# Prompt attention by head pairs, expert sums by TensorE, input weights loaded one stage earlier

## The chip, the cores and the metric

One Trainium2 chip, one of its cores. The metric is the device time of the kernel in microseconds (us); all data are float32. The core's engines are named as in the profile: PE (TensorE matmul), PEld (TensorE weight load), DVE (VectorE), ACT (ScalarE), POOL (GpSimd) and SP (SyncE, which here only starts DMAs). Each engine takes its instructions strictly in the order of its own list and waits on semaphores that other engines raise.

## What is computed

One layer of a decoder, for a prompt of 1024 tokens and for 8 single-token sequences with a past of 8192. What the change touches, cut from the reference (prompt side):

```python
mod = (silu(c) @ w_ada + b_ada)                    # stage_ada
h @ w_in                                           # stage_in: D 1024 -> 2536 columns

def mla_attend(q_nope, q_rope, k_nope, k_rope, c_kv, key_pos, q_pos, w_uv):   # 8 heads
    s = (q_nope @ k_nope + q_rope @ k_rope) * MLA_SCALE
    s = where(key_pos <= q_pos, s, -inf)
    p = softmax(s)
    ...                                            # p @ values, 64 columns a head

def dsa_attend(q, k_sel, v_sel, sel_pos, valid, q_pos, rel_bias):             # 8 heads
    s = q @ k_sel * DSA_SCALE + bias               # only the 256 selected keys are valid
    p = softmax(s)
    return p @ v_sel                               # 64 columns a head

x = x + gate_a * (concat(mla, dsa) @ w_out)        # stage_out
x = x + gate_f * (sum over 6 experts of gate * y_expert + shared expert)      # stage_combine
```

## The kernel before

`build` runs nine stages one after another, with a barrier of all engines between them: ada, in, index, prompt, sample, out, dispatch, routed, combine. The prompt is handled in `NT` = 8 tiles of 128 tokens; tile `NT` is the 8 samples. A float32 matmul is recorded as two MATMUL instructions, a transpose by the identity as one.

**stage_ada** (L190) streams `w_ada` through `NW` = 4 buffers of 3 MB. **stage_in** (L299) then loads `w_in` as five column groups from SP's list (L349), the second x tile between the first and the second, and after the groups the smaller weights and the third x tile. For each tile PE turns x, multiplies by five groups of `w_in` (`project`, L497), and ACT takes each result out of one of two PSUM banks (`take`, L429). ACT's list has `norm_x(2)`, which needs the third x tile, ahead of `take(0, 0)`.

**attend** (L794) is the last part of the prompt stage. An item `n` is one head of one block of 128 queries: for each block `i` (0 to 7) the 8 heads of MLA (`g` = 0) and the 8 of DSA (`g` = 1), 128 items. Causality is used, so block `i` has w = 128 (i+1) keys. For an item:

- `scores` (PE, L902): query as weights, keys streamed, into PSUM `pS[n % 2]`, two banks an item. It waits for `s_nm` of item n-2, that is, until DVE is done with that pair of banks.
- `scale_and_max` (DVE, L1011, L1016): adds mask or bias, writes `S`, and gives the row's maximum.
- `exps` (ACT, L957): exponential and row sum, into `Pr`.
- `turn` (PE, L912): transposes of `Pr` in groups of up to four, into `pT[group % 2]`; a group needs the copy of the group two before it.
- `evac` (DVE L946 for even groups, ACT L944 for odd ones): copies a group to `PT`.
- `pv` (PE, L923): a 128x128 block of `PT` as weights, 64 columns of values streamed, into `pO[n % 2]`.
- `norm` (DVE, L1021, L1025): reciprocal of the sum, and the scaled result to `O`, stored to `omix` with tokens in rows.

An item has one group when i < 4 and two when i is 4 or more. The order in each list is written out by hand:

```python
# PE                          # DVE                        # ACT
scores(n + 1)                 scale_and_max(n + 1)         exps(n + 1)
turn(n)                       evac(dve, n, 0)              evac(act, n, 1)
pv(n - 1)                     norm(n - 1)
                              select(...)  # one step of the key selection of the next block
```

**stage_out** (L2037): for each tile PE turns the mixed rows (`turn_mix`, L2101), ACT copies them to `mT`, PE multiplies by `w_out` (`out`, L2113), DVE scales and adds x; then the router. `turn_mix(t + 1)` stands ahead of `out(t)`, and SP starts the load of the second tile after the two loads of `w_out`.

**stage_combine** (L2728): for each tile POOL gathers six rows of 4 KB a token, one for each chosen expert (L2749), DVE multiplies each by its gate and adds (L2776, L2778), multiplies by `gate_f` (L2780), POOL adds to `z` (L2756), and ACT starts the store. POOL's list has the addition of tile t ahead of the gathers of tile t+3.

Of the kernel before, what the change touches and what calls it, by code (L numbers as in the profile page):

```python
# [128 lines left out]

def build(nc, T):  # L130
    root = ExitStack()
    with root:
# [33 lines left out]
        for st in (stage_ada, stage_in, stage_index, stage_prompt, stage_sample, stage_out, stage_dispatch, stage_routed,  # L166
                   stage_combine):
            stage_name[0] = st.__name__[6:] + "_"
            if st is stage_out:
                G["z"] = sb("z", [P, NT + 1, D])  # L170
            with ExitStack() as ctx:
                st(nc, T, G, sem, *alloc(ctx))

            nc.clear_and_free_semaphores(list(sem_cache.values()))
            nc.all_engine_barrier()
            sem_cache.clear()
# [13 lines left out]
def stage_ada(nc, T, G, sem, sb, ps):  # L190
# [3 lines left out]
    NW = 4  # L194
# [13 lines left out]
    with nc.Block() as block:  # L208
# [25 lines left out]
        def _(act):  # L234
            act.wait_ge(s_c, 64)
            act.activation(sc[:, :], cs[:, :], ACT.Sigmoid).then_inc(s_sc, 1)

# [61 lines left out]
def stage_in(nc, T, G, sem, sb, ps):  # L299
# [5 lines left out]
    Win = sb("Win", [P, KD, D_IN])  # L305
# [23 lines left out]
    cols = [(0, 512), (512, 1024), (1024, 1536), (1536, 2048), (2048, D_IN)]  # L329
    s_ss, s_rs, s_xn, s_t, s_h, s_p, s_e, s_eps, s_b, s_w2, s_v = (  # L330
        sem("in_" + n) for n in ("ss", "rstd", "xn", "t", "h", "p", "evac", "eps", "b", "weights", "v"))
    s_x, s_wc, s_cs = sem("in_x"), [sem(f"in_w{g}") for g in range(5)], [sem("in_cs0"), sem("in_cs1")]
# [4 lines left out]
    with nc.Block() as block:  # L337
        @block.sync
        def _(sp):
# [8 lines left out]
            for g, (a, b) in enumerate(cols):  # L348
                sp.dma_start(Win[:, :, a:b], T["w_in"][0, :, a:b].rearrange("(k p) n -> p k n", p=P)).then_inc(s_wc[g], 16)  # L349
                if g == 0:  # L350
                    load(1)
# [205 lines left out]
        def _(dve):  # L557
# [99 lines left out]
            root_x(0)  # L657
            root_x(1)
            scale_h(0)
# [134 lines left out]
def attend(nc, T, G, sem, sb, ps, U, thr, FIRST, widths, at):  # L794
# [10 lines left out]
    S = [sb(f"S{i}", [P, SEQ]) for i in range(2)]  # L805
    Pr = [sb(f"Pr{i}", [P, SEQ]) for i in range(2)]
    PT = [sb(f"PT{i}", [P, NT, P]) for i in range(2)]
    O = [sb(f"O{i}", [P, D]) for i in range(2)]
    mx = sb("mx", [P, 4, 2])
    rs = sb("rs", [P, 2])  # L810
    mxp = sb("mxp", [P, 2, 4])
    eq, rank, ones = sb("eq", [P, SEQ]), sb("rank", [P, SEQ]), sb("onesrow", [P, SEQ])
# [4 lines left out]
    names = ("S", "nm", "P", "T", "evd", "eva", "O", "on", "row", "mb", "st", "mx", "v", "fin", "bi")  # L817
    s_S, s_nm, s_P, s_T, s_evd, s_eva, s_O, s_on, s_row, s_mb, s_st, s_mx, s_v, s_fin, s_bi = (sem("at_" + n) for n in names)
# [10 lines left out]
    def by_dve(upto):  # L829
        return (upto + 1) // 2  # L830

    with nc.Block() as block:
        @block.sync
        def _(sp):
            def store(i):
                sp.wait_ge(s_on, 16 * (i + 1))
                sp.dma_start(T["omix"][i * P:(i + 1) * P, :], O[i % 2][:, :]).then_inc(s_out[i % 2], 16)

# [15 lines left out]
            t = bias_rows(T)  # L854
            sp.dma_start(bias[:, :, :], bass.AP(t.tensor, t.offset + P - 1, [[H * 384 - 1, P], [384, H], [1, 2 * P]])).then_inc(s_bi, 16)
# [4 lines left out]
            for i in range(2, NT):  # L860
                sp.wait_ge(s_S, 16 * (i - 1))
# [8 lines left out]
        def _(pool):  # L870
# [4 lines left out]
            for i in range(NT):  # L875
                if i >= 2:
                    pool.wait_ge(s_nm, 16 * (i - 1))
# [8 lines left out]
        def _(pe):  # L886
            def scores(n):
                i, g, h = items[n]
                if g == 0 and h == 0:
# [4 lines left out]
                if n >= 2:  # L894
                    pe.wait_ge(s_nm, n - 1)
                w = widths[i]
                b = 64 * (h % 2)
                q = qm[i % 2][0:QK, h, :] if g == 0 else qd[i % 2][b:b + 64, h // 2, :]
                for z in range(0, w, 512):
                    e = min(z + 512, w)  # L900
                    k = kmT[0:QK, h, z:e] if g == 0 else kdT[b:b + 64, h // 2, z:e]
                    m = pe.matmul(pS[n % 2][z // 512][:, 0:e - z], q, k, start=True, stop=True)  # L902
                m.then_inc(s_S, 1)

            def turn(n):
                pe.wait_ge(s_P, n + 1)
                for gi in range(gfirst[n], gfirst[n + 1]):
                    _, b0, cnt = groups[gi]
                    if gi >= 2:
                        pe.wait_ge(s_evd if gi % 2 == 0 else s_eva, gi // 2)  # L910
                    for b in range(cnt):
                        m = pe.transpose(pT[gi % 2][:, b * P:(b + 1) * P], Pr[n % 2][:, (b0 + b) * P:(b0 + b + 1) * P], c("ident"))  # L912
                    m.then_inc(s_T, 1)

            def pv(n):
                i, g, h = items[n]
                pe.wait_ge(s_evd, by_dve(gfirst[n + 1]))
                if gfirst[n + 1] >= 2:
                    pe.wait_ge(s_eva, gfirst[n + 1] // 2)
                if n >= 2:  # L920
                    pe.wait_ge(s_on, n - 1)
                for j in range(i + 1):
                    m = pe.matmul(pO[n % 2][:, 0:64], PT[n % 2][:, j, :], V[g][:, j, h * 64:h * 64 + 64], start=(j == 0), stop=(j == i))  # L923
# [3 lines left out]
            for n in range(len(items)):  # L927
                if n + 1 < len(items):
# [4 lines left out]
            pv(len(items) - 1)  # L933

        def evac(eng, n, odd):
            for gi in range(gfirst[n], gfirst[n + 1]):
                if gi % 2 == odd:
                    _, b0, cnt = groups[gi]
                    eng.wait_ge(s_T, gi + 1)
                    if n >= 2:  # L940
# [1878 lines left out]
```

## Time and profile before

| | us |
|---|---|
| median of 3 runs (3324.84 to 3331.28) | 3330.16 |
| the profiled execution | 3362.59 |
| its span in the trace | 3360.8 |
| PE busy | 2749.1 (82%) |
| DVE busy | 1640.3 (49%) |
| ACT busy | 1053.7 (31%) |
| POOL busy | 379.3 (11%) |

The profiled execution is one run of its own, recorded by the hardware; its span is the time from the first to the last recorded instruction. Its time is 32 us above the median of the unprofiled runs. Busy shares are averages over nine stages with different limits, so the stage is read, not the average. PE's granted clock is one of two levels, 2.4 GHz (1.0 in the profile) or 1.2 GHz (0.5); over a longer stretch the profile shows their mean.

### The profile page before, as it was taken

What the parts mean: (1) busy time and instruction counts of PE and PEld (TensorE: products, weight loads), DVE (VectorE), ACT (ScalarE), POOL (GpSimd) and SP (SyncE); (2) the same over time, 40 slices, a digit from 0 to 9 for tenths busy, and PEclk for the clock granted to TensorE, in tenths of its full rate; (3) what the DMA queues carried; (4) which work ended last, traced back from release to release, by engine and by line L of the source; (5) the groups of instructions that cost most, each with busy time, mean ns of one, the idle gap of its engine ahead of it and who ended that gap; (6) DMA issues with size and microseconds to landing.
All of it is one profiled execution on the core that took longest, in us unless ns stands there. A gap on an engine that the chain in (4) does not pass through costs nothing. (4 is left out here: it accounts for less than half of the span.)

```text
span 3360.8 us, 42372 instructions
## 1 busy us (share of the span) xinstructions
PE 2749.1 (82%) x14194; PEld 1585.7 (47%) x14194; DVE 1640.3 (49%) x3931; ACT 1053.7 (31%) x2214; POOL 379.3 (11%) x373
## 2 busy tenths in 40 slices
PE   4699996869898989699997447978688899999950
PEld 1344434458786878576775403534233333333310
DVE  0255554668687787656775852267111111111138
ACT  0122223559696877533332001122011111111100
POOL 0000001011000101011010130015100000100037
PEclk8899997879998999857998768989799999999975
DMA  8412225132170202050001124120989977887866
GB/s 323 173 56 79 68 66 217 35 120 75 60 243 20 99 28 76 19 151 29 15 21 68 40 78 167 58 101 13 348 336 339 387 263 289 328 310 262 295 249 223
DMA packets 230771, 514.83 MB, mean 153 GB/s; under 512 B 23269, under 2 KB 84911, under 8 KB 223184
## 3 DMA queue, kind: packets, MB, share of 16 engines
q1 hardware_dynamic: 190580, 344.31, 29.4%
q0 software_dynamic: 29648, 130.76, 10.8%
q10 hardware_dynamic: 10388, 37.79, 2.8%
q8 instruction: 86, 1.41, 0.2%
q14 instruction: 69, 0.57, 0.1%
HBM read 622.40 MB, written 87.02 MB: 211 GB/s over the span
## 5 line engine op out<-in xcount | busy, mean ns | idle before, releaser
L2619 PE MATMUL routed_ex_pG<-routed_ex_WG,routed_ex_XT 128*64 128x512 f32 x2048 | 487.9, 620 | 72.8 <-DMA routed_ex_WG<-in_w_e_gu 31.0
L1771 DVE TENSOR_REDUCE ssqc<-SQ 128x8 f32<-128x512 f32 x516 | 346.2, 683 | 134.4 <-ACT SQ L1577 121.7
L2711 DVE COPY routed_ex_XT<-routed_ex_pX 128x512 f32<-128x512 f32 x128 | 85.6, 689 | 507.4 <-PE routed_ex_pX L2606 507.4
L1492 PE MATMUL eK<-WA,LT 128*128 128x272 f32 x1032 | 329.8, 402 | 0.0
L1489 PE MATMUL eK<-dWkv,LT 128*128 128x256 f32 x1032 | 318.6, 391 | 10.2 <-ACT SQ L1577 9.7
L497 PE MATMUL in_pp<-in_Win,in_hT 128*128 128x512 f32 (+3 forms) x720 | 313.4, 593 | 12.0 <-ACT in_pr L429 12.0
L1577 ACT ACTIVATE SQ<-eK 128x512 f32<-128x512 f32 x516 | 292.0, 603 | 58.5 <-PE eK L1492 42.3
L2619 PEld LDWEIGHTS routed_ex_pG<-routed_ex_WG,routed_ex_XT 128*64 128x64 f32 x2048 | 141.1, 141 | 331.6 <-issue 308.3
L2639 PE MATMUL routed_ex_pY<-routed_ex_WD,routed_ex_AT 128*64 128x512 f32 x1024 | 232.4, 595 | 0.0
L1492 PEld LDWEIGHTS eK<-WA,LT 128*128 128x128 f32 x1032 | 202.1, 196 | 29.4 <-DVE numc L1770 0.2
L497 PEld LDWEIGHTS in_pp<-in_Win,in_hT 128*128 128x128 f32 (+1 forms) x720 | 128.9, 181 | 184.1 <-issue 184.0
L1489 PEld LDWEIGHTS eK<-dWkv,LT 128*128 128x128 f32 x1032 | 191.3, 197 | 46.2 <-ACT SQ L1577 14.8
L957 ACT ACTIVATE Pr<-S,mx 128x128 f32<-128x128 f32 (+7 forms) x128 | 99.2, 775 | 281.5 <-DVE mx L1016 281.5
L1533 ACT ACTIVATE ujunk<-W,unb 128x384 bf16<-128x384 int16 (+5 forms) x192 | 169.5, 883 | 16.7 <-DVEq L1596 16.1
L2672 ACT ACTIVATE routed_ex_sg<-routed_ex_pG 128x256 f32<-128x256 f32 x64 | 24.6, 384 | 435.6 <-PE routed_ex_pG L2619 435.6
L2714 DVE TENSOR_TENSOR routed_ex_sg<-routed_ex_sg,routed_ex_pG 128x256 f32<-128x256 f32 x64 | 26.6, 416 | 252.0 <-ACT routed_ex_sg L2672 252.0
L2639 PEld LDWEIGHTS routed_ex_pY<-routed_ex_WD,routed_ex_AT 128*64 128x64 f32 x1024 | 70.8, 137 | 133.5 <-issue 133.5
L2113 PE MATMUL out_oY<-out_Wo,out_mT 128*128 128x512 f32 (+1 forms) x288 | 126.7, 598 | 0.7 <-DVE out_z L2193 0.7
L1551 ACT ACTIVATE LT<-eT 128x512 f32<-128x512 f32 x168 | 98.4, 585 | 89.1 <-PE eT L1458 88.9
L2683 ACT ACTIVATE routed_ex_Y<-routed_ex_pY 128x512 f32<-128x512 f32 x128 | 76.5, 597 | 158.2 <-PE routed_ex_pY L2639 158.2
L912 PE MATMUL aT<-K,Pr 128*128 128x128 f32 x576 | 101.5, 307 | 2.1 <-ACT Pr L957 1.8
L912 PEld LDWEIGHTS aT<-K,Pr 128*128 128x128 f32 x576 | 73.0, 154 | 62.5 <-issue 45.0
(516 smaller groups left out, 4030.9 us busy)
## 6 DMA issues: line engine op xcount, KB each, us to landing
routed_ex_WG<-in_w_e_gu SPq DMA_DIRECT2D x128, 2048.0 KB
routed_ex_WD<-in_w_e_down SPq DMA_DIRECT2D x128, 1024.0 KB
s_yblk<-routed_ex_Y ACTq DMA_DIRECT2D x64, 512.0 KB
ada_Wada<-in_w_ada SPq DMA_DIRECT2D x8, 3072.0 KB, 27.6
s_yblk<-zrows SPq DMA_DIRECT2D x15, 1024.0 KB
in_Win<-in_w_in SPq DMA_DIRECT2D x4, 2048.0 KB
s_tdT<-in_td SPq DMA_DIRECT2D x8, 832.0 KB
s_h<-out_h POOLq DMA_DIRECT2D x9, 512.0 KB
```

The costliest lines, as they stand in the source:

```text
L497: m = pe.matmul(pp[n % 2][0:R, 0:b - a], hT[t % 2][:, k, 0:R], Win[:, k, a:b], start=(k == 0), stop=(k == KD - 1))
L912: m = pe.transpose(pT[gi % 2][:, b * P:(b + 1) * P], Pr[n % 2][:, (b0 + b) * P:(b0 + b + 1) * P], c("ident"))
L957: act.activation(Pr[n % 2][:, 0:w], S[n % 2][:, 0:w], ACT.Exp, bias=mx[:, n % 4, 0:1], accum_out=mx[:, n % 4, 1:2]).then_inc(s_P, 1)
L1489: pe.matmul(pK[kn % 3][:, 512 + z:512 + z + HK], key, Wkv[:, 4:8, 0:NOPE], start=True, stop=True)
L1492: pe.matmul(pK[kn % 3][:, z:z + HK + 16], key, WA[:, pr, :], start=True, stop=True).then_inc(s_KN, 1)
L1533: act.activation(ujunk[:, 0:w], hi16[:, a:a + w] if i < 16 else flat[:, a:a + w], ACT.Sign, bias=nb[:, j:j + 1], accum_out=cu[:, j:j + 1]) ...
L1551: act.activation(LT[u % 3][0:r, 0:cnt * P], pT[0:r, 0:cnt * P], ACT.Copy).then_inc(s_ev, 1)
L1577: act.activation(SQ[kn % 4].rearrange("p (a n) -> p a n", a=2), pK[kn % 3][:, :].rearrange("p (a n) -> p a n", a=2)[:, :, z:z + HK], ACT.S ...
L1771: dve.tensor_reduce(ssqc[cg % 2][:, n - 1 - tau, :], SQ[kn % 4].rearrange("p (h d) -> p h d", h=H), AX.X, ALU.add).then_inc(s_red, 1)
L2113: m = pe.matmul(pY[n][0:R, :], mT[t % 2][:, k, 0:R], Wo[:, k, n * 512:(n + 1) * 512], start=(k == 0), stop=(k == KD - 1))
L2619: m = pe.matmul(pG[u][r, :], XT[u][:, k, r], WG[2 * u + v][:, k, :], start=(k == 0), stop=(k == KD - 1))
L2639: m = pe.matmul(pY[n][r, :], AT[u][:, k, r], WD[2 * u + v][:, k, n * 512:(n + 1) * 512], start=(k == 0), stop=(k == 1))
```

## The change

- **ada and in:** room for `w_in` is made at the start of stage_ada (`NW` becomes 3), and ACT starts its five loads there, once the last piece of `w_ada` has landed. In stage_in DVE's `scale_h(0)` stands ahead of `root_x(1)`.
- **attend:** an item is now a pair of heads, 64 items. `scores` writes the two heads to `pS[0]` and `pS[1]`; all four banks belong to one item, so it waits for `s_nm` of item n-1. For DSA the two heads lie in the two row halves of the array, alternating. `exps` writes in place. `turn` has two groups an item when i < 4 and four when i is 4 or more, and one more group (a = -1) that spreads the reciprocals of the item before: its two matmuls put `1/sum` in rows. `pv` has 64 columns of values as weights, one head in each column half, and 128 columns of `PT` streamed. Copies are divided one to DVE, two to ACT (`x % 3 == 0` is DVE's). The result has channels in rows and goes to `mixT`. The four steps of `select` hold what seven did. The bias load moves from SP to ACT.
- **stage_out:** loads `mT` directly; only the 8 sample rows are still turned.
- **stage_combine:** gates times the identity (ACT) are weights of matmuls that sum four of the six experts in PSUM; DVE does the other two, adds the sum, and adds to `z` itself. SP starts the stores.

```diff
-    NW = 4
+    NW = 3
@@ stage_ada, ACT
+            act.wait_ge(s_w[(KD - 1) % NW], 16 * ((KD - 1) // NW + 1))
+            for (a, b), s in zip(in_cols(), G["s_win"]):
+                act.dma_start(G["Win"][:, :, a:b], T["w_in"][0, :, a:b]...).then_inc(s, 16)
@@ stage_in, SP
-            for g, (a, b) in enumerate(cols):
-                sp.dma_start(Win[:, :, a:b], ...).then_inc(s_wc[g], 16)
-                if g == 0:
-                    load(1)
+            load(1)
@@ attend
-    items = [(i, g, h) for i in range(NT) for g in range(2) for h in range(H)]
+    items = [(i, g, p) for i in range(NT) for g in range(2) for p in range(H // 2)]
+    NI = len(items)
+    for n in range(NI + 1):
         gfirst.append(len(groups))
-        groups += [(n, b, min(4, i + 1 - b)) for b in range(0, i + 1, 4)]
+        if n < NI:
+            groups += [(a, b, min(4, i + 1 - b)) for a in range(2) for b in range(0, i + 1, 4)]
+        if n:
+            groups.append((-1, 0, 1))
+    on_dve = [a >= 0 and x % 3 == 0 for x, (a, b, cnt) in enumerate(groups)]
@@ PE
             def scores(n):
-                if n >= 2:
-                    pe.wait_ge(s_nm, n - 1)
+                if n:
+                    pe.wait_ge(s_nm, n)
                 for z in range(0, w, 512):
+                    for a in range(2):
+                        h, r = 2 * p + a, slice(64 * a, 64 * a + 64)
+                        q = qm[i % 2][0:QK, h, :] if g == 0 else qd[i % 2][r, p, :]
+                        k = kmT[0:QK, h, z:e] if g == 0 else kdT[r, p, z:e]
+                        m = pe.matmul(pS[a][z // 512][:, 0:e - z], q, k, start=True, stop=True)
             def turn(n):
+                if n < NI:
+                    pe.wait_ge(s_P, n + 1)
+                for x in range(gfirst[n], gfirst[n + 1]):
+                    a, b0, cnt = groups[x]
+                    if x >= 2:
+                        evacuated(pe, x - 1)
+                    if a < 0:
+                        pe.wait_ge(s_rs, n)
+                        for b in range(2):
+                            m = pe.matmul(pT[x % 2][64 * b:64 * b + 64, 0:P], rs[:, (n - 1) % 2, b:b + 1].to_broadcast([P, 64]), c("ident"), ...)
+                    else:
+                        for b in range(cnt):
+                            m = pe.transpose(pT[x % 2][:, b * P:(b + 1) * P], S[n % 2][a][:, ...], c("ident"))
             def pv(n):
                 for j in range(i + 1):
-                    m = pe.matmul(pO[n % 2][:, 0:64], PT[n % 2][:, j, :], V[g][:, j, h * 64:h * 64 + 64], ...)
+                    for a in range(2):
+                        m = pe.matmul(pO[n % 2][64 * a:64 * a + 64, 0:P], V[g][:, j, h * 64:h * 64 + 64], PT[n % 2][a][:, j, :], ...)
@@ ACT: order kept
             exps(0)
-            for n in range(len(items)):
+            for n in range(NI + 1):
+                if n + 1 < NI:
                     exps(n + 1)
-                evac(act, n, 1)
+                evac(act, n, False)
@@ DVE
-            for n, (i, g, h) in enumerate(items):
+            for n in range(NI + 1):
                     scale_and_max(n + 1)
-                evac(dve, n, 0)
+                evac(dve, n, True)
+                    invert(n)
                     norm(n - 1)
@@ stage_out
-                sp.dma_start(mi[t % 2][0:R, :], T["omix"][t * P:t * P + R, :]).then_inc(s_in[t % 2], 16)
+                    sp.dma_start(mT[t % 2][:, :, :], T["mixT"][:, t * P:(t + 1) * P]...).then_inc(s_in[t % 2], 16)
-                    turn_mix(*tiles()[t + 1])
+                if t == 1:
+                    turn_sample()
                 out(t, R)
@@ stage_combine
+                for k in range(NV, TK):
+                    a = act.activation(W[t % 2][0:R, k - NV, 0:R], c("ident")[0:R, 0:R], ACT.Copy, scale=G["gate"][0:R, t, k:k + 1])
+                for n in range(2):
+                    for k in range(NV, TK):
+                        m = pe.matmul(pS[t % 2][n][0:R, :], W[t % 2][0:R, k - NV, 0:R], E[t % NE_][0:R, k, n * 512:(n + 1) * 512], ...)
-                pool.tensor_tensor(z[0:R, t, :], z[0:R, t, :], acc[t % 2][0:R, :], ALU.add).then_inc(s_z, 1)
+                dve.tensor_tensor(z[0:R, t, :], z[0:R, t, :], a, ALU.add).then_inc(s_z, 1)
```

## Rows read from the trace of the kernel before

**Rows 1.** Busy time by stretch of the attention: PE, PEld, DVE, ACT, POOL, granted clock, DMA.
```profile
1430.70:1557.00 126.30, 125.32 (x419) 92.65 (x419) 70.94 (x312) 38.85 (x129) 15.87 (x4) 0.50 0.38 103
1557.00:1828.30 271.30, 269.56 (x1696) 204.89 (x1694) 193.31 (x680) 103.17 (x224) 18.12 (x4) 1.00 0.05 16
```

**Rows 2.** Instructions in order of time (start, length): one MLA head, block 6.
```profile
1704.32 0.69 DVE L1011 CUSTOM_DVE_ANT_0 S<-aS,open_row 128x512 f32<-128x512 f32 x1 [1.08 <-PE aS L902]
...
1704.93 0.55 DVE L1011 CUSTOM_DVE_ANT_0 S<-aS,open_row 128x384 f32<-128x384 f32 x1
...
1705.61 0.69 DVE L946 COPY PT<-aT 128x512 f32<-128x512 f32 x1
1705.72 1.04 ACT L957 ACTIVATE Pr<-S,mx 128x896 f32<-128x896 f32 x1 [2.33 <-DVE mx L1016]
...
1706.39 1.72 PE L902 MATMUL aS<-kmTs,qmt 96*128 96x512 f32 x4
...
1706.76 0.47 ACT L944 ACTIVATE PT<-aT 128x384 f32<-128x384 f32 x1
...
1707.95 0.93 PE L912 MATMUL aT<-K,Pr 128*128 128x128 f32 x7
...
1708.71 1.67 PE L923 MATMUL aO<-vmS,PT 128*128 128x64 f32 x14
...
1710.22 1.72 PE L902 MATMUL aS<-kmTs,qmt 96*128 96x512 f32 x4
```

**Rows 3.** ACT's exponentials by form (ns: min, median, max), and one copy.
```profile
L957 ACT ACTIVATE Pr<-S,mx x128: 395/775/1151, 1432.2 to 1821.8; 128x128 f32<-128x128 f32 x16, 128x256 f32<-128x256 f32 x16, 128x384 f32<-128x384 f32 x16, 128x512 f32<-128x512 f32 x16
...
1799.58 0.58 ACT L944 ACTIVATE PT<-aT 128x512 f32<-128x512 f32 x1
```

**Rows 4.** Groups by line (busy us, mean ns): full array, column halves, row halves.
```profile
L497 PE MATMUL in_pp<-in_Win,in_hT 128*128 128x512 f32 (+3 forms) x720 | 313.4, 593 | 12.0 <-ACT in_pr L429 12.0
L2639 PE MATMUL routed_ex_pY<-routed_ex_WD,routed_ex_AT 128*64 128x512 f32 x1024 | 232.4, 595 | 0.0
L742 PE MATMUL iS<-kiT,qi 64*128 64x512 f32 (+3 forms) x160 | 39.4, 627 | 16.1 <-ACT rl L759 9.7 <-DMA qi<-s_tdT 6.1
```

**Rows 5.** Bursts with gaps in stage_ada: the group's row, and one stretch.
```profile
L253 PE MATMUL ada_pm<-ada_Wada,ada_cT 128*9 128x512 f32 x192 | 36.9, 930 | 26.9 <-DMA ada_Wada<-in_w_ada 26.9
...
40.00:50.00 10.00, 6.79 (x40) 1.42 (x44) 0.00 (x0) 0.00 (x0) 0.00 (x0) 0.73 1.00 429
```

**Rows 6.** Start of stage_in: a stretch before it, then instructions in order of time.
```profile
70.00:75.00 5.00, 4.75 (x24) 0.63 (x16) 0.11 (x1) 0.00 (x0) 0.00 (x0) 0.50 0.00 0
...
115.84 0.48 SPq L345 DMA_DIRECT2D in_x<-in_x_prompt  x1
...
123.61 1.06 ACT L407 ACTIVATE in_xn<-in_x 128x1024 f32<-128x1024 f32 x1 [27.13 <-DMA in_x<-in_x_prompt]
...
127.09 21.96 PE L497 MATMUL in_pp<-in_Win,in_hT 128*128 128x512 f32 x48 [12.00 <-ACT in_pr L429]
```

**Rows 7.** Start of stage_out, instructions in order of time.
```profile
2040.23 1.97 PE L2101 MATMUL out_oT<-K,out_mi 128*128 128x128 f32 x8 [11.96 <-DMA out_mi<-s_omix]
...
2049.78 1.23 DVE L2180 SCALAR_TENSOR_TENSOR out_r_cf<-out_r_cf,out_gfr 128x1024 f32<-128x1024 f32 x1 [25.92 <-DMA out_Wr<-in_w_router]
...
2058.93 13.97 PE L2113 MATMUL out_oY<-out_Wo,out_mT 128*128 128x512 f32 x32 [0.73 <-DVE out_z L2193]
```

**Rows 8.** stage_combine: the stretch, its densest part, and three kinds of instruction.
```profile
3244.00:3360.80 116.80, 0.00 (x0) 0.00 (x0) 91.00 (x63) 0.00 (x0) 87.03 (x63) 0.50 0.72 258
...
3256.00:3260.00 4.00, 0.00 (x0) 0.00 (x0) 3.02 (x3) 0.00 (x0) 3.19 (x3) 0.50 1.02 414
...
3276.71 8.52 DVE L2778 SCALAR_TENSOR_TENSOR combine_cacc<-combine_cE,gate,combine_cacc 128x1024 f32<-128x1024 f32 x5
...
3280.13 2.70 POOL L2756 TENSOR_TENSOR out_z<-out_z,combine_cacc 128x1024 f32<-128x1024 f32 x1
...
L2749 POOL DMA_INDIRECT combine_cE<-s_yblk,slot x54: 937/1016/1773, 3244.4 to 3337.9; - x54
```

More of the change, by code:

```diff
@@ L168, in build @@
             stage_name[0] = st.__name__[6:] + "_"
+            if st is stage_ada:
+                weights_in = root.enter_context(ExitStack())
+                G["Win"] = alloc(weights_in)[0]("Win", [P, KD, D_IN])
+                G["s_win"] = [nc.alloc_semaphore(f"win{g}") for g in range(len(in_cols()))]
             if st is stage_out:
@@ L804, in attend @@
     mb = [sb(f"mb{i}", [P, H, 2 * P]) for i in range(2)]
[L805 to L812, printed above, removed]
+    S = [[sb(f"S{i}{a}", [P, SEQ]) for a in range(2)] for i in range(2)]
+    PT = [[sb(f"PT{i}{a}", [P, NT, P]) for a in range(2)] for i in range(2)]
+    O = [sb(f"O{i}", [P, KD, P]) for i in range(2)]
+    RB = [sb(f"RB{i}", [P, P]) for i in range(2)]
+    mx, sm, rs = sb("mx", [P, 2, 2]), sb("sm", [P, 2, 2]), sb("rs", [P, 2, 2])
+    mxp = sb("mxp", [P, 2, 2, 4])
+    eq, rank, ones = sb("eq", [P, SEQ]), sb("rank", [P, SEQ]), sb("onecol", [P, 1])
     more = sb("more", [P, NT - FIRST])
@@ L1015, in scale_and_max @@
-                dve.wait_ge(s_mx, nmx[0])
-                dve.tensor_reduce(mx[:, n % 4, 0:1], mxp[:, k, 0:len(parts)], AX.X, ALU.max, negate=True).then_inc(s_nm, 1)
+                for a in range(2):
+                    for x, (z, e) in enumerate(parts):
+                        if g == 0:
+                            m = open_row[:, SEQ - w + z:SEQ - w + e]
+                        elif z >= w - near:
+                            dve.wait_ge(s_mb, i + 1)
+                            m = mb[i % 2][:, 2 * p + a, 2 * P - w + z:2 * P - w + e]
+                        else:
+                            m = U[:, at[i] + z:at[i] + e]
+                        zb = z // 512
+                        dve.tensor_tensor_reduce(out=S[k][a][:, z:e], in0=pS[a][zb][:, z - 512 * zb:e - 512 * zb], in1=m,
+                                                 scale=MLA_SCALE if g == 0 else DSA_SCALE, scalar=NEG, op0=ALU.add, op1=ALU.max,
+                                                 accum_out=mxp[:, k, a, x:x + 1]).then_inc(s_mx, 1)
+                        nmx[0] += 1
@@ L1028, in _ @@
             scale_and_max(0)
-            for n, (i, g, h) in enumerate(items):
-                if n + 1 < len(items):
+            for n in range(NI + 1):
+                if n + 1 < NI:
                     scale_and_max(n + 1)
-                evac(dve, n, 0)
+                evac(dve, n, True)
+                if n < NI:
+                    invert(n)
                 if n:
                     norm(n - 1)
-                if g == 1 and FIRST <= i + 1 < NT:
-                    select(i + 1 - FIRST, h)
@@ L1037, in _ @@
-            norm(len(items) - 1)
+                if n < NI:
+                    i, g, p = items[n]
+                    if g == 1 and FIRST <= i + 1 < NT:
+                        select(i + 1 - FIRST, p)
 def scoped(nc):
@@ L2043, in stage_out @@
     gf = sb("gfr", [P, D])
-    mi = [sb(f"mi{i}", [P, D]) for i in range(2)]
+    mi = sb("mi", [NS, D])
     xi = [sb(f"xi{i}", [P, D]) for i in range(2)]
@@ L2728, in stage_combine @@
 def stage_combine(nc, T, G, sem, sb, ps):
+    c = G["c"]
     NE_ = 3
+    NV = 2
     z = G["z"]
```

262 lines of the change are left out of this document (134 added, 128 removed).

## The prediction

> **What bounds the kernel now.** I read the slices of the whole span first: PE is busy in nearly all of it, and the change touches four places, so each is read by itself: busy time by stretch, then the instructions in order of time, to see which wait ends last there.
>
> The attention takes 397.6 us (1430.7 to 1828.3) and is bound by PE: busy 125.3 of 126.3 us while the clock is 0.5, and 269.6 of 271.3 us while it is 1.0; DVE is busy 264 us in all, ACT 142 [rows 1]. Block 6 shows the rhythm: a head takes from one start of scores to the next 1710.22 - 1706.39 = 3.83 us, of which scores 1.56, seven transposes 0.76 (0.109 each) and `pv` 1.51 (0.108 for each of 14 records) [rows 2]. No gap lies between them. The reader should also see the order on the other engines: ACT's exponentials start at 1705.72, its copy of the *earlier* head's group only at 1706.76, after them; DVE's copy at 1705.61 stands behind the scale-and-max of 1704.32 [rows 2]. This lateness costs nothing now, because a head has at most two groups and there are two `pT` banks: a group only needs the copy of a group of the head before.
>
> stage_in waits at its start for a DMA, stage_out likewise, and stage_combine is shared between POOL (87 of 117 us), DVE (91 us) and DMA (share 0.72) [rows 6 to 8].
>
> **Attention, PE's work.** Column halves: 1024 records of 512 columns in halves have a busy time of 232.4 us, 0.227 each, against 313.4/720 = 0.435 for the full array, so two halves run side by side [rows 4]. Row halves: the indexer's scores do 160 records in 39.4 us, 0.246 each with mixed widths and clocks, which also says side by side [rows 4]. So the DSA scores of a pair cost what one head costs, and `pv` of a pair costs 0.214 for each key block (two records of 128 streamed columns, as 128 columns cost 0.109 in a transpose) instead of 4 x 0.108 = 0.432. No row shows the column halves with so short a stream; the bounds are 0.214 (full overlap, taken, as in the nearest row) and 0.43 (none). At the full clock PE's work for 64 pairs is then 236 us. A head's scores over the eight blocks sum to 8.1 us (w x 1.667 ns and 0.035 for each 512 columns begun, which gives the 1.56 of block 6), twelve times (8 MLA, 4 for the DSA pairs) 97; 576 transposes 63; `pv` 8 x 36 x 0.214 = 62; reciprocals 64 x 0.22 = 14. The old kernel sums to 130 + 63 + 124 = 317. If PE stayed the bound, some 80 us would go.
>
> **Attention, the waits.** It does not stay the bound. An item now has three groups for i < 4 and five for i of 4 and more, and still two `pT` banks. PE's third group of item n therefore needs the copy of the first group of the *same* item. That copy stands on DVE behind `scale_and_max(n+1)`, or on ACT behind `exps(n+1)`, which itself waits for `scale_and_max(n+1)`, which waits for `scores(n+1)`. And `pv(n-1)` and `scores(n+2)` are queued on PE behind the third group. `scores(n+2)` could not be earlier anyway than the end of `scale_and_max(n+1)`, as all four banks are one item's. So a pair costs a chain in which nearly nothing overlaps. For block 6, MLA, clock 1.0:
>
> - scores of two heads 2 x 1.56 = 3.12; to DVE 0.20
> - scale and max of two heads: 1704.32 to 1705.72 is 1.40 for one, the second adds 0.61 + 0.48 = 1.09: 2.5 [rows 2]
> - two exponentials of 1.04 and the read of the sum: 2.2 [rows 2, 3]
> - two copies on ACT (first group, third group) one after the other, 0.58 each: 1.16 [rows 3]
> - reciprocals and three handovers: 0.47
> - `pv`: 7 x 0.214 = 1.50.
>
> Together 11.1 us for a pair, against 2 x 3.83 = 7.67. DSA saves one head's scores: 9.7. The same sum for the other blocks (scores as above; scale 1.04 ns a column and 0.08 a part; exponential 0.29 + 0.84 ns a column, which are the ends 395 and 1151 of [rows 3]; one copy of 0.26 to 0.58 for i < 4) gives, MLA/DSA: 3.2/3.0, 4.5/4.0, 5.7/5.2, 6.9/6.2, 8.9/7.9, 10.0/8.6, 11.1/9.7, 12.2/10.6; four pairs of each are 471 us. The selection steps stand on DVE ahead of the next scale-and-max: some 0.6 us for each of 24 pairs, 15 us. So 486 us if the clock is 1.0 throughout.
>
> **The clock.** In the first 126 us it is 0.5 although PE is busy all the time [rows 1]. The change makes PE less busy there, so I keep 0.5 for i < 4: the PE terms double, 522 + 15 = 537 us. For i of 4 and more PE would work in bursts (`pv` and scores, 5 us) with gaps of some 5 us (scale, exponentials). The nearest rows for such a pattern are stage_ada's: PE busy 6.8 of 10 us, clock 0.73 on average, yet its records take 930 ns where 593 is usual [rows 4, 5]: the bursts run mostly at the low level, and the high level comes when the burst is over. At 0.5 throughout (16.0 and 13.0 for block 6) the chain sums to 644 + 18 = 662 us. The bounds are thus 537 and 662; I take the middle, 600, since the longer MLA bursts should reach the high level before they end and the DSA bursts hardly. Against 398 that is +202 us.
>
> The Trainium skill says the same from its side: TensorE: Matmul & The Clock Gate, "A second HAM failure mode: psum-queue depth-cycling", describes a kernel that cycles through PSUM banks, idles shortly between groups of matmuls and drops again and again to the lower clock. By that rule the sum would go towards 662; by the attention's own second stretch (1.0 without a break) towards 537.
>
> **stage_ada and stage_in.** The DMA engines move nothing from 70 to 75 us [rows 6], while the last piece is used; the five loads (10 MB, at the 429 GB/s of [rows 5] some 25 us) start there, 11 us earlier than now. One buffer fewer costs nothing while two loads of 3 MB remain outstanding. What goes: PE's wait of 12.0 us at 115 to 127, behind ACT, behind the third x tile, whose load SP could issue only at 115.84 after the weights [rows 6]; and 1 to 4 us at the first projection. Against it: x(0) and the stores of `mod` share the DMA engines with `w_in`, 1 to 3 us, and one more clearing of semaphores, under 1. Taken: -11 (0 to -16).
>
> **stage_out.** The first `out` waits now for the turn of tile 1, landed only at 2040.2; but then tile 0's x1 waits for the router weights until 2049.78, and the second `out` starts at 2058.93 behind it [rows 7]. The DMA order of these constants hardly moves, so of the 10 us at the first `out` some 4 remain. Eight turns of 8 x 0.109 = 0.9 us go from PE: 7. Taken: -11 (-5 to -15). The loads of `mT` in pieces of 512 B have a whole `out` (14 us) to land in.
>
> **stage_combine.** DVE is busy 91 us for nine tiles now, 10.1 a tile; a product with addition costs 8.52/5 = 1.7 [rows 8]. Five such passes remain at most (two products, the sum from PSUM, `gate_f`, `z`), the first shorter: 6.0 to 8.5. POOL loses nine additions of 2.70 = 24 us. PE needs 16 records of 0.435 = 7.0 a tile (13.9 at the low clock). What is late next is the DMA: 258 GB/s x 116.8 us = 30.1 MB, at the 414 GB/s of its densest part 73 us; POOL's 54 gathers at 1.25 us are 68 [rows 8]. From 3244 that is 3320, then two tiles' tail of DVE and a store, 16: 3339 to 3345 instead of 3360.8. Taken: -18 (-8 to -22; if PE stays at the low clock, 9 tiles x 13.9 = 125 us, and nothing is gained).
>
> **Sum.** +202 - 11 - 11 - 18 = +162 us on the profiled execution's 3362.6: 3525. Unprofiled runs lie 32 us lower (median 3330.2): 3492.
>
> **The rivals.**
> 1. *The clock stays high.* Attention 486 to 537: +48 to +99 us, 3380 to 3430. For it: after 1557 it never fell [rows 1]. Against: PE was never idle there. Chance 0.17.
> 2. *Short streams in column halves do not overlap, and the clock is low.* `pv` doubles, 288 x 0.214 = 62 us at full clock, more at half: attention 660 to 700, 3550 to 3590. For it: no row has such short streams. Against: the halves of L2639. Chance 0.15.
> 3. *Faster.* The place is the third group of `turn`: if its copy comes before PE needs it, PE stays the bound at 236 to 304 us, the attention takes about 300, and the whole 3330 - 98 - 40 = 3190. It decides from the break-even: the attention may take 398 + 40 = 438 us, so PE's waits a pair must stay below (438 - 304)/64 = 2.1 us; I count 3 to 6. For it: DVE and ACT have room on average (264 and 142 of 398 us). Against: both lists are in fixed order. Chance 0.07.
> 4. *The forecast*, 3492, its own range 3430 to 3550: chance 0.61.
>
> The measurement of this kernel can tell about 0.2% from no change (7 us). Faster by more: 0.08 (rival 3 and a rest); within: 0.02; slower: 0.90. The range that leaves out no more than 2 in 10 is 3400 to 3570: it takes in half of rival 1 and half of rival 2.
>
> **What would show it.** In the changed kernel: a timeline of block 6 with PE idle between the second and the third group of an item, ended by a copy on ACT that starts right after two exponentials; a pair of MLA heads taking 11 to 16 us and one of DSA 10 to 13; PE busy well under 80% in the attention, and clock records that change between the levels for i of 4 and more. `pv` records of a pair at 0.107 on average at the full clock show the column halves right. stage_in without the 12 us wait, combine ending some 100 us after its start. Wrong would be: PE busy over 90% in the attention (rival 3), or the third group released by anything that stands ahead of the exponentials.

## The result, and the profile after

| | us, median (lowest to highest) | ratio to before (95%) |
|---|---|---|
| before | 3330.72 (3324.84 to 3342.41), 4 runs | |
| after | 3517.12 (3513.49 to 3517.84), 4 runs | 1.0549 (1.0514 to 1.0584): slower |

The forecast was 3492.0 (3400 to 3570) with 0.90 for slower. The profiled execution of the changed kernel took 3516.81 us, 0.3 us from its median; its span is 3515.0 us, against 3360.8 before: 154.2 more. By stage, from the two traces:

| stretch | before | after | change | forecast |
|---|---|---|---|---|
| start to the first scores of the attention | 1430.8 | 1423.1 | -7.7 | -11 |
| attention, first scores to last normalisation | 397.5 | 585.1 | +187.6 | +202 |
| sample attention between | | | +2 | 0 |
| last sample store to the first matmul of stage_dispatch | 204.5 | 200.5 | -4.0 | -11 |
| stage_dispatch and the routed experts | 1013.8 | 1009.7 | -4.1 | 0 |
| stage_combine | 122.1 | 102.4 | -19.7 | -18 |

The attention of the changed kernel by stretch (start and end, length, then busy us and instructions of PE, PEld, DVE, ACT and POOL, granted clock, DMA share, GB/s); the cut at 1611 is where block 4 begins:

```profile
1423.10:1611.00 187.90, 127.98 (x689) 83.96 (x690) 70.06 (x306) 56.60 (x189) 15.84 (x4) 0.64 0.24 68
1611.00:2008.20 397.20, 256.10 (x1680) 187.00 (x1679) 133.07 (x474) 113.61 (x249) 18.06 (x4) 0.79 0.03 9
```

Beside [rows 1]: PE did slightly less work in busy time (384 against 395 us), but where it was busy 99% of the time before it is now busy 66%, and in the second stretch, where the clock was 1.00, it is 0.79. DVE was relieved (203 against 264 us), ACT loaded (170 against 142). No engine is full. The same place as [rows 2], block 6, MLA, in order of time (start, length; in brackets the idle time before and what ended it):

```profile
1829.37 0.93 PE L941 MATMUL aT<-K,S 128*128 128x128 f32 x7
...
1829.57 0.69 DVE L1045 CUSTOM_DVE_ANT_0 S<-aS,open_row 128x512 f32<-128x512 f32 x1 [3.19 <-PE aS L924]
...
1831.87 0.16 DVE L1050 TENSOR_REDUCE mx<-mxp 128x2 f32<-128x4 f32 x1
...
1832.07 1.04 ACT L993 ACTIVATE S<-S,mx 128x896 f32<-128x896 f32 x1 [8.68 <-DVE mx L1050]
...
1833.11 1.03 ACT L993 ACTIVATE S<-S,mx 128x896 f32<-128x896 f32 x1
...
1834.13 0.57 ACT L980 ACTIVATE PT<-aT 128x512 f32<-128x512 f32 x1
...
1834.85 1.73 PE L941 MATMUL aT<-K,S 128*128 128x128 f32 x7 [4.55 <-ACT PT L980]
...
1837.12 3.23 PE L952 MATMUL aO<-PT,vmS 128*64 128x128 f32 x28
...
1840.28 1.77 PE L924 MATMUL aS<-kdTs,qdt 64*128 64x512 f32 x8
```

The first group of transposes is ready at about 1830, and ACT is idle (8.68 us up to 1832.07), but does not copy it: its queue has the exponentials of the next item first, and these wait for the maximum on DVE, which is there at 1832.03. The copy comes at 1834.13, right behind the two exponentials, and PE, idle 4.55 us, goes on at 1834.85. The clock in stretches of 3 us of this window:

```profile
1828.00:1831.00 3.00, 2.30 (x12) 1.40 (x10) 1.43 (x5) 0.00 (x0) 0.00 (x0) 1.00 0.00 0
1831.00:1834.00 3.00, 0.00 (x0) 0.00 (x0) 1.55 (x7) 1.93 (x3) 0.00 (x0) 0.90 0.00 0
1834.00:1837.00 3.00, 2.05 (x11) 1.71 (x13) 0.00 (x0) 1.69 (x5) 0.00 (x0) 0.50 0.00 0
1837.00:1840.00 3.00, 3.00 (x32) 2.95 (x28) 0.00 (x0) 0.39 (x2) 0.00 (x0) 0.50 0.00 0
1840.00:1843.00 3.00, 2.97 (x19) 1.44 (x15) 1.19 (x6) 0.00 (x0) 0.00 (x0) 0.96 0.00 0
1843.00:1846.00 3.00, 0.00 (x0) 0.00 (x0) 1.68 (x11) 1.25 (x3) 0.00 (x0) 1.00 0.00 0
```

PE is granted a clock of 0.90 and 1.00 in the gaps in which it does nothing (1831 to 1834, 1843 to 1846), and the low one, 1.2 GHz, in the first part of the burst behind the gap (1834 to 1840); in the last 3 us of the burst it is 0.96 again. The Trainium skill (TensorE: Matmul & The Clock Gate, "A second HAM failure mode: psum-queue depth-cycling") describes such a swing for groups of matmuls with short idles; by that rule, the trace agrees. In its case the median matmul still runs at the full speed; here the measurement differs, as most of the burst itself is slow: the `pv` of this item takes 3.23 us for 28 records, where at 1.00 the 32 of block 7 take 1.92 us (at 2004.01 in the same trace).

What PE waits for in the attention, and the group that waits most, in the changed kernel (first part: us in total, times, longest; second: busy us, mean ns, idle time before, and what ended it):

```profile
PE aT L941 <- ACT PT L980: 105.9, 32, 5.4
PE aT L938 <- issue: 53.7, 29, 3.5
PE aT L941 <- DVE PT L978: 24.7, 10, 2.9
```

```profile
L941 PE MATMUL aT<-K,S 128*128 128x128 f32 x576 | 110.0, 338 | 130.6 <-ACT PT L980 105.9 <-DVE PT L978 24.7
L952 PE MATMUL aO<-PT,vdS 128*64 128x128 f32 x576 | 62.3, 390 | 0.0
L952 PE MATMUL aO<-PT,vmS 128*64 128x128 f32 x576 | 59.4, 376 | 0.0
L938 PE MATMUL aT<-K,rs 128*64 128x128 f32 x256 | 41.1, 412 | 68.8 <-issue 53.7 <-DVE PT L978 14.2
```

Idle time ended by ACT's copies, 105.9 us, is more than half of the 187.6 that the attention lost. L938 is the group of the reciprocals, which for i < 4 is an item's third group. The two lines of `turn` together have 130.6 + 68.8 = 199.4 us of PE's 201 idle us; for 53.7 of them the profile names no releaser. The other three places (stage_in against [rows 6], stage_out against [rows 7], stage_combine against [rows 8]), in order of time:

```profile
68.38 16.21 ACTq L251 DMA_DIRECT2D ada_Win<-in_w_in  x5
...
91.93 1.06 ACT L419 ACTIVATE in_xn<-in_x 128x1024 f32<-128x1024 f32 x1 [83.67 <-DMA in_x<-in_x_prompt]
...
2215.67 15.68 PE L2157 MATMUL out_oY<-out_Wo,out_mT 128*128 128x512 f32 x32 [14.01 <-DMA out_Wo<-in_w_out]
2233.04 1.23 DVE L2220 SCALAR_TENSOR_TENSOR out_r_cf<-out_r_cf,out_gfr 128x1024 f32<-128x1024 f32 x1 [27.15 <-DMA out_Wr<-in_w_router]
...
2238.44 16.24 PE L2157 MATMUL out_oY<-out_Wo,out_mT 128*128 128x512 f32 x32 [6.49 <-DVE out_z L2233]
...
3429.49 23.21 PE L2821 MATMUL combine_cS<-combine_cE,combine_cW 128*128 128x512 f32 x48 [17.69 <-DMA combine_cE<-s_yblk,slot]
```

### The profile page after: what moved, and what is told of

Read it like the earlier page. It is cut to its first block and busy times, and to the rows that moved or that the text cites. A ratio compares the mean times of both kernels' runs of the same rounds, so it can differ in the third digit from the quotient of the medians.

```text
span 3515.0 us, 43036 instructions
## 1 busy us (share of the span) xinstructions
PE 2796.2 (80%) x14530; PEld 1577.5 (45%) x14530; DVE 1539.2 (44%) x3708; ACT 1085.0 (31%) x2319; POOL 348.0 (10%) x364
## 5 line engine op out<-in xcount | busy, mean ns | idle before, releaser
L509 PE MATMUL in_pp<-ada_Win,in_hT 128*128 128x512 f32 (+3 forms) x720 | 312.2, 591 | 0.0
L941 PE MATMUL aT<-K,S 128*128 128x128 f32 x576 | 110.0, 338 | 130.6 <-ACT PT L980 105.9
L993 ACT ACTIVATE S<-S,mx 128x128 f32<-128x128 f32 (+7 forms) x128 | 98.3, 769 | 367.6 <-DVE mx L1050 367.6
L509 PEld LDWEIGHTS in_pp<-ada_Win,in_hT 128*128 128x128 f32 (+1 forms) x720 | 128.5, 181 | 171.3 <-issue 171.1
L941 PEld LDWEIGHTS aT<-K,S 128*128 128x128 f32 x576 | 82.7, 173 | 170.4 <-issue 141.4
```

The source lines that it names most:

```text
L509: m = pe.matmul(pp[n % 2][0:R, 0:b - a], hT[t % 2][:, k, 0:R], Win[:, k, a:b], start=(k == 0), stop=(k == KD - 1))
L941: m = pe.transpose(pT[x % 2][:, b * P:(b + 1) * P], S[n % 2][a][:, (b0 + b) * P:(b0 + b + 1) * P], c("ident"))
L993: m = act.activation(S[n % 2][a][:, 0:w], S[n % 2][a][:, 0:w], ACT.Exp, bias=mx[:, n % 2, a:a + 1], accum_out=sm[:, n % 2, a:a + 1])
```

## The experiments

The windows quoted have the columns of the first fence; each is the whole attention of its kernel. Baseline of the first four experiments: before 3333.95 us in 9 runs (each ratio is against runs on the same chip).

**e1: ACT copies first.** In ACT's list:

```diff
             for n in range(NI + 1):
+                evac(act, n, False)
                 if n + 1 < NI:
                     exps(n + 1)
-                evac(act, n, False)
```

> The changed kernel, with ACT's copies of item n ahead of the exponentials of item n+1 in ACT's list; nothing else moves. Theory (the chain): PE's third group waits for a copy that stands behind the exponentials of the next item, so the two exponentials (0.9 to 2.4 us a pair) lie on the path of every pair. They leave it: the attention falls from 585 us to about 435, the whole from 3517 to about 3370 (3330 to 3400), and PE's wait at the transposes is then ended mainly by DVE's copies. Rival A (the four score banks of one item: PE waits for scale-and-max anyway): the exponentials were hidden, the whole stays within 15 us of 3517. Rival B (the low clock is the whole loss): PE's work is unchanged, so the time falls only as far as the clock rises, less than 60 us.

Measured: 3312.43 us (3308.51 to 3314.2), ratio 0.9927 (0.9899 to 0.9954).

```profile
1424.70:1808.00 383.30, 307.79 (x2368) 213.31 (x2368) 201.81 (x778) 172.36 (x438) 33.83 (x8) 0.90 0.15 43
```

```profile
1679.82 0.93 PE L941 MATMUL aT<-K,S 128*128 128x128 f32 x7
...
1680.46 0.60 ACT L980 ACTIVATE PT<-aT 128x512 f32<-128x512 f32 x1 [4.74 <-PE aT L941]
...
1681.20 0.63 PE L941 MATMUL aT<-K,S 128*128 128x128 f32 x4 [0.45 <-ACT PT L980]
```

Two lines change places, and at this place 4.55 us of idle time become 0.45. The attention falls by 202 us, and the whole from 5.5% above the kernel before to 0.7% below it, a small gain but clear of the noise. The 202 us can be told apart by PE's row: its idle time falls from 201 to 75.5 us, that is by 125.5, and its busy time for the same records from 384 to 308, that is by 76, with the mean clock at 0.90 instead of 0.74. The idle time that went is more than the exponentials themselves, which last some 100 us for all 64 pairs (128 x 0.29 and 0.84 ns a column, the ends in [rows 3]); the copy had also stood behind their wait for the scale-and-max. The wait costs twice: once as idle time, once as the low clock of what follows.

As expected, what is left of the wait is ended mainly by DVE's copies (first line, against ACT's in the second):

```profile
PE aT L941 <- DVE PT L978: 36.0, 20, 2.9
PE aT L941 <- ACT PT L980: 11.8, 23, 0.7
```

DVE's list has the same flaw, its copies standing behind `scale_and_max(n + 1)`; no run exchanges those two.

**e2: PE's `pv` first**, and **e3: both.** In PE's list the values of the item before go ahead of the transposes, which fills the wait instead of taking it away:

```diff
                     scores(n + 1)
-                turn(n)
                 if n:
                     pv(n - 1)
+                turn(n)
```

> The changed kernel, with the value matmuls of item n-1 ahead of the transposes of item n in PE's list; nothing else moves. Theory (the chain): they move from behind the last group to the time in which PE waits for scale-and-max and the exponentials, so their 0.2 to 1.7 us a pair (twice that at the low clock) leave the path: the attention 585 to about 495, the whole about 3430 (3400 to 3455). Rival (PE's waits are for the score banks, not in the order of the list): within 15 us of 3517.

> The two reorderings together. Theory (the chain): both terms leave the path, PE gets to 60 to 75% in the attention, and it takes 405 us if the clock goes on changing between its levels, 320 if it stays high: the whole 3335 or 3250, so between the kernel before (3331) and 80 us below it. Rival (DVE, with scale-and-max ahead of its copies, binds as soon as ACT is out of the way): the second reordering adds nothing to the first, 3370.

Measured: e2 3439.87 (3433.49 to 3440.74), ratio 1.031 (1.0274 to 1.0347); e3 3284.97 (3283.92 to 3286.41), ratio 0.9852 (0.9819 to 0.9886). Their attention, and PE's largest wait in e2:

```profile
1423.70:1931.80 508.10, 387.17 (x2368) 236.63 (x2368) 205.31 (x778) 170.07 (x438) 33.89 (x8) 0.77 0.12 33
```

```profile
1420.50:1779.00 358.50, 310.13 (x2368) 197.66 (x2368) 204.60 (x778) 171.01 (x438) 34.01 (x8) 0.92 0.16 46
```

```profile
PE aT L941 <- ACT PT L980: 68.7, 29, 3.8
```

Filling the wait with `pv` gives 77 us and leaves the clock at 0.77; taking it away gives 202; both 227. They overlap: `pv` hides a wait that e1 has removed already. e2 is inside its range (3400 to 3455); e3 lies between its two figures (3335 and 3250), with PE busy 87% of the attention where 60 to 75% was expected.

**e4: `pv` without column halves side by side.** The same 1152 records, but one head's all before the other's:

```diff
-                for j in range(i + 1):
-                    for a in range(2):
+                for a in range(2):
+                    for j in range(i + 1):
```

> The changed kernel, with the value matmuls of the one head all ahead of those of the other, so that two in a row use the same column half. Theory (short streams in the two column halves run side by side when they alternate): the value matmuls, 116 us busy in the attention now, need nearly twice that; the attention grows by 60 us (high clock) to 125 (low), the whole to about 3600. Rival (with 128 streamed columns the halves gain nothing, the loads of the weights bound them): within 15 us of 3517.

Measured: 3553.06 (3548.14 to 3554.14), ratio 1.065 (1.0613 to 1.0687).

The attention; its last `pv`, in order of time; and `pv` by group (busy us, mean ns, idle time before):

```profile
1421.30:2048.80 627.50, 424.37 (x2368) 315.74 (x2368) 202.93 (x778) 169.84 (x438) 33.88 (x8) 0.75 0.09 26
```

```profile
2045.54 2.73 PE L952 MATMUL aO<-PT,vdS 128*64 128x128 f32 x27
```

```profile
L952 PE MATMUL aO<-PT,vmS 128*64 128x128 f32 x576 | 85.3, 363 | 0.0
...
L952 PE MATMUL aO<-PT,vdS 128*64 128x128 f32 x576 | 81.3, 351 | 0.0
```

`pv` is busy 166.6 us instead of 121.7, and the attention takes 42 us more. In that last stretch the clock is 1.00 and a record takes 2.73/27 = 0.101 us; in the changed kernel 32 alternated records take 1.92 at the same clock, 0.060 each. So two column halves, used in turn, do work side by side with streams of 128 columns, and rival 2 falls. Whether it is the streams that overlap, or the load of the weights of one half with the stream of the other, no run separates. The price is below the expected 60 to 125 us.

**e5: work added in the gap.** In blocks 4 to 7, ahead of the third group's wait, four matmuls whose result nobody reads (384 columns each, into a part of `pO` that is not read):

```diff
                     a, b0, cnt = groups[x]
+                    if x == gfirst[n] + 2 and 4 * H <= n < NI:
+                        if n >= 2:
+                            pe.wait_ge(s_on, n - 1)
+                        for _ in range(4):
+                            pe.matmul(pO[n % 2][:, P:512], c("ident")[0:QK, :], kmT[0:QK, 0, 0:384], start=True, stop=True)
```

> The changed kernel with work added: for blocks 4 to 7 PE does four matmuls of 384 columns (96 rows of the identity against the first head's keys) into an unused part of the value bank, ahead of each item's third group, where it now waits for a copy; their results are used nowhere. They are 2.6 us a pair at the high clock, 5.1 at the low one, 82 to 164 us in all, into waits of 4.5 to 5.5 us a pair. Theory (the low clock costs part of the 585 us, and comes from PE's gaps): the granted clock in blocks 4 to 7 goes to near 1.0, the matmuls of the path get shorter, and the attention falls in spite of more work, 585 to about 530 (500 to 560); the whole about 3465. Rival A (the level in blocks 4 to 7 costs nothing on the path, which is made of DVE's and ACT's times): the added work fills waits only, within 15 us of 3517. Rival B (the level does not follow the gaps): added work at the low clock overruns the wait: 3530 to 3600.

Measured: 3484.1 (3478.89 to 3488.29), ratio 1.0465 (1.0427 to 1.0503), so 33 us faster than the changed kernel with 128 matmuls (256 records) more. All of the attention, and its blocks 4 to 7, which begin here at 1605.5 with the scores of block 4:

```profile
1421.80:1972.70 550.90, 422.33 (x2624) 282.59 (x2624) 202.93 (x778) 169.50 (x438) 33.95 (x8) 0.84 0.11 30
1605.50:1972.70 367.20, 300.98 (x1938) 202.30 (x1936) 133.35 (x474) 113.06 (x249) 18.10 (x4) 0.91 0.04 10
```

The useful data and order are the changed kernel's; one wait, that for the scaled result of item n-2, comes a little earlier in PE's list. PE is busy 82% of blocks 4 to 7 instead of 64%, the clock rises from 0.79 to 0.91, and the 397 us become 367. (Blocks 0 to 3, which are not changed, take 183.7 us instead of 187.5 in these two traces.) The attention, 550.9 us, is inside the expected 500 to 560. This shows by itself that a part of the loss, about 30 us at least, is the clock and not the wait. What is left is the chain through DVE and ACT, which no clock of PE shortens.

**e6: three `pT` banks**, and **e7: e3 and e6 together.** The two outputs share one bank, so that a third is free for transposes; a group then needs the copy of the third-last group:

```diff
-    pT = [ps("aT0"), ps("aT1")]
-    pO = [ps("aO0"), ps("aO1")]
+    pT = [ps("aT0"), ps("aT1"), ps("aT2")]
+    pOb = ps("aO0")
+    pO = [pOb[:, 0:P], pOb[:, 2 * P:3 * P]]
...
-                    if x >= 2:
-                        evacuated(pe, x - 1)
+                    if x >= 3:
+                        evacuated(pe, x - 2)
...
-                if n >= 2:
-                    pe.wait_ge(s_on, n - 1)
+                if n:
+                    pe.wait_ge(s_on, n)
```

> The changed kernel with three transpose banks instead of two: the two value results share one bank, so the value matmuls of item n wait for the scaled result of item n-1; a group then needs the copy of the group three before it. The lists keep their order. Theory (the third group of an item waits for a copy of the same item): for blocks 0 to 3, three groups an item, no group needs a copy of its own item any more, and these blocks get from 188 us to about 140; for blocks 4 to 7 the fourth of five groups still does: the attention about 490 (450 to 520), the whole about 3425. Rival A (the four score banks hold PE back, not the transposes): within 15 us of 3517. Rival B (the shared value bank is a new wait): slower than 3517.

> The two reorderings of the run at 3285 us together with the three transpose banks. Theory (chain): PE's remaining waits at the transposes, 22 + 22 us, go for the most part; the attention 358 to about 325 (295 to 345), the whole about 3250. Rival (PE is bound by the score banks now, scores after scale-and-max): no more than 10 us less than 3285. Rival (shared value bank, the scaled result waits on ACT's copy of the reciprocals and PE on it): slower than 3285.

Measured (before here: 3329.48, 7 runs, as for e5 and e8): e6 3417.75 (3410.95 to 3425.95), ratio 1.0267 (1.0225 to 1.0309); e7 3246.19 (3239.21 to 3249.97), ratio 0.9745 (0.9707 to 0.9783), the fastest version. The attention of e6 and the first scores of its block 4; the attention of e7; then e7's scores, `pv` and transposes of block 7 in order of time:

```profile
1422.20:1904.40 482.20, 338.76 (x2368) 239.53 (x2368) 200.47 (x778) 165.48 (x438) 33.91 (x8) 0.83 0.12 34
...
1565.33 2.94 PE L925 MATMUL aS<-kmTs,qmt 96*128 96x512 f32 x8
```

```profile
1422.60:1740.10 317.50, 300.40 (x2368) 194.32 (x2368) 204.32 (x778) 170.18 (x438) 34.08 (x8) 0.93 0.18 52
```

```profile
1689.75 3.70 PE L925 MATMUL aS<-kmTs,qmt 96*128 96x512 f32 x8
...
1693.38 1.97 PE L953 MATMUL aO<-PT,vmS 128*64 128x128 f32 x32
...
1695.28 2.06 PE L942 MATMUL aT<-K,S 128*128 128x128 f32 x16
...
1697.64 3.70 PE L925 MATMUL aS<-kmTs,qmt 96*128 96x512 f32 x8
```

A third bank alone gives 103 us. Blocks 0 to 3, where no group needs a copy of its own item any more, fall from 187.5 to 143 us (1422.2 to 1565.3; expected 140). An item of blocks 4 to 7 has five groups, so the fourth still meets the late copy (PE still waits 97.1 us for ACT's copies). The attention of both runs is inside its expected range. With the right order on both engines it gives another 41 us over e3, and PE is busy 95% of the attention: 1689.75 to 1697.64, 7.9 us a pair, without a gap.

**e8: the old attention and `out` with the new stage_ada, stage_in and stage_combine.**

> The kernel before, with the new stage_ada and stage_in and the new stage_combine alone; attention and stage_out as before. Theory (the parts add up): -8 and -20 us, measured from one trace each: 3331 to about 3303 (3295 to 3310). Rival (the attention's slowness is partly left over from the earlier stages' changes, or the stages' gains hang on the new attention): outside 3290 to 3320.

Measured: 3298.55 (3297.71 to 3299.29), ratio 0.9904 (0.9869 to 0.994). Its attention, and that part of it with a low clock:

```profile
1418.00:1789.20 371.20, 367.11 (x2112) 277.31 (x2112) 263.16 (x992) 142.03 (x352) 34.00 (x8) 0.91 0.16 47
...
1418.00:1489.70 71.70, 70.79 (x263) 53.98 (x264) 46.00 (x214) 25.87 (x94) 11.36 (x3) 0.55 0.58 167
```

The edits of stage_ada and stage_in and of stage_combine are worth 31 us together (20 to 44 by the interval), as expected (3295 to 3310), and the rest of the change costs 3517.12 - 3298.55 = 219 us. The stretch also shows something about the execution profiled before: the same lists of instructions took 397.5 us there and 371.2 here, with PE busy 99% of the time in both; what differs is the clock, which stayed low for 126 us [rows 1] there and for about 72 here.

## Why the prediction was right, and where its terms were off

**The mechanism** (third group of `turn` behind a copy that stands behind the next item's exponentials) was right. The timeline has every link at its place, and e1, which changes nothing but that order, removes 202 us of attention. Rival 3 (faster) had the right place and the right condition; its copy came late as counted (PE idle 201/64 = 3.1 us a pair, against 3 to 6 counted and a break-even of 2.1).

**The size of the attention**: forecast +202, by the two traces +188. In block 6 the exponentials of one pair start 13.5, 13.6 and 13.2 us before those of the next (MLA), and 13.2, 11.9 and 13.4 (DSA): on average 13.4, in the middle of 11.1 to 16.0, and 12.8, near the upper end of 9.7 to 13.0. So DSA is nearer to MLA than forecast; its `pv` costs it as much as MLA's, 3.20 us for 28 records (at 1888.37) against the 3.23 in the rows above. By stretch: blocks 0 to 3 took 187.9 us where the forecast's own sum has 206 (155 at the full clock, 51 more at the low one), as their clock was 0.64 and not 0.5; blocks 4 to 7 took 397.2, where some 390 were left of the 600. The middle between 537 and 662 was a choice and not worked out; that 585 lies so near to it is partly luck, as blocks 0 to 3 were taken too dear and DSA too cheap.

**The clock** was right as a pattern: low in the first part of a burst, high at its end and in the gap. It was too small in one respect: I took it as a price on top of the chain, and it feeds back. That showed when the wait went: e1 was expected to take 150 us off the attention, to some 3370 us, and took off 202, to 3312. Of these the idle time is 125.5 and the busy time 76, and the expectation had credited it the exponentials and only some 50 us more.

**Column halves**: 32 records in 1.97 us and 28 in 1.75 at the full clock, so a key block adds 0.22 us (both in e7, the second at 1685.71); forecast 0.214. The prediction's sign "records at 0.107 on average" was counted wrongly: a key block of a pair is four records in the trace, and 0.214 is then 0.054 each. The sum used the right figure.

**PE's own work** was mis-sized: 236 us at the full clock for 64 pairs. e7, nearly without waits, has 300.4 us at a mean clock of 0.93, an estimate of some 280 at the full clock. The reciprocals' broadcast takes 0.44 us a pair (1689.38 in e7, 4 records) and not 0.22, and the groups of transposes and `pv` carry their start-up: 16 transposes take 2.06 us, not 16 x 0.109 = 1.74. In the changed kernel this is small beside the waits and the clock; rival 3's own figure would have been too low by it (attention 300; e7 has 317.5).

**stage_in**: forecast -11, measured -7.7 up to the first scores. The 12 us wait is gone, as forecast; but x(0) is normalised at 91.93 against 85.73 before and the first projection starts at 105.85 against 99.72, 6 us later. The rows tell the 6 us apart. ACT issues the five loads for 16.21 us (68.38 to 84.59), and the next stage begins only behind them: SP issues the load of x(0) at 85.51 where it did at 81.94, although DVE and PE were done 1.9 us earlier than before. That is 3.6 us, and the prediction had no term for it. From its issue to its use x(0) then takes 6.4 us instead of 3.8, the 1 to 3 us that I had allowed for sharing the DMA engines. The last projection starts at 499.2 against 506.2.

**stage_out**: forecast -11, measured -4 in the traces, the term that was off most for its size. The first `out` starts 10.8 us after the stage's first DMA where it was 19.1, but the second only 2.5 us earlier (33.5 against 36.0): it waits for tile 0's x1, that for the router weights (27.15 us of DVE's idle time, 25.92 before [rows 7]). The prediction named this wait and left 4 us of the gain; 2.5 remained. And behind this wait, 6.49 us long, the second `out` starts at the low clock:

```profile
2238.40:2241.40 3.00, 2.96 (x4) 1.45 (x5) 0.19 (x2) 2.72 (x4) 0.00 (x0) 0.50 0.59 175
```

It takes 16.24 us where before, behind an idle time of 0.73, it took 13.97 [rows 7]. The turns that went do show: a later tile takes 17.40 us (2258.13 to 2275.53) instead of 18.23 (2077.22 to 2095.45 before), 0.83 each, 5 us for six tiles. From the stage's first DMA to the last matmul of `out` it is 176.1 us before and 171.0 after, 5 us less: 2.5 and 5 gained, 2.3 lost by the clock. From the end of the attention on it is 370.7 before, 370.6 in e8 and 367.7 after, since the sample attention between took 2 us more.

**stage_combine**: forecast -18, measured -19.7. PE works 70.2 us for 144 records, and the 54 gathers of POOL are issued from 3419.1 to 3492.3; the term of PE is right (16 records take 7.10 us, forecast 7.0), but the bound is the DMA, which the prediction had as what comes next: the first records wait 17.69 us for it, a tile takes 8.87 us (3472.00 to 3480.87), and in this stretch the DMA share is 1.02 at the full clock:

```profile
3460.00:3490.00 30.00, 22.33 (x51) 9.17 (x50) 21.65 (x23) 3.85 (x12) 23.60 (x22) 1.00 1.02 412
```

**The offset**: I subtracted 32 us because the profiled execution of before lay so much above its median. Most of it (26.3 us) is the low clock of its attention, if e8's attention is taken as the usual one. The other runs of before point the same way: their span follows their mean clock, 3319.8 us at 0.904, 3328.5 at 0.901 and 3341.3 at 0.898, against 3360.8 at 0.891 for the profiled one. The changed kernel has no such excess: its profiled execution is at its median. So the forecast of 3525 for a profiled execution stands against 3516.8 measured, and against a usual run of before the attention costs not 188 but 585.1 - 371.2 = 214 us. The 25 us between 3492 and 3517 are then: attention 12, stage_in 3, stage_out 7, stage_combine -2, the stages between -2, and the 6 of the offset that e8's attention does not account for.

What is not settled: why the same lists keep the low clock for 126 us in one execution and 72 in another, and how much of the 125.5 us of idle time that e1 removes was itself made longer by the low clock. e5 gives a lower bound for the clock in four blocks, no more.

## What to carry to other kernels

When items grow from two groups to five and the buffers between two engines stay two, look in every engine's list for what stands ahead of the copy that frees the buffer. If it is work of the *next* item, the lookahead has become a serial chain, and exchanging two lines may be worth more than the change itself: here 205 us, where the attention's change is worth 54 even in its best version (317.5 us in e7 against 371.2 in e8). Average load does not show this (DVE and ACT were busy 35% and 29% of the attention), and a gap in TensorE's work had to be priced twice here, as idle time and as the slower burst behind it; it did so again in stage_out.

## What the runs showed of the hardware that was not expected

- Work without use made the kernel faster: 128 matmuls (256 records) added in the gaps, 33 us less (e5), clock 0.91 instead of 0.79 in the four blocks.
- The full clock was granted in the gaps (1.00 and 0.90 with PE busy 0.00 us of 3) and the low one in the first 6 us of the burst behind; its last 3 us had 0.96.
- The attention of before, PE busy 99% of the time, took 397.5 us in one execution and 371.2 us in another kernel with the same lists, at mean clocks of 0.84 and 0.91.
- Two streams of 128 columns in column halves, alternated, take 0.060 us a record at the full clock; the same records one half after the other 0.101.
